# Query tiles inside the row norm, feed-forward tiles inside the output stage, and an earlier store of the last keys

## The reference

```
xn   = rmsnorm(x, norm1_w)
proj = xn @ w_in                  # q, k, v, forget logits, z, xBC, dt, two gates
q, k = headwise rmsnorm(q), headwise rmsnorm(k)      # 16 heads of 64
...                               # attention, state-space scan, branches -> merged
x = x + merged @ w_out
h = rmsnorm(x, norm2_w)
x = x + square(relu(h @ w_up)) @ w_down              # 1024 -> 4096 -> 1024
```

## Time and profile before

| what | value |
|---|---|
| median of 3 runs | 2817.95 us (2816.93 to 2821.05) |
| profiled execution | 2824.97 us |
| span of the profiled execution | 2823.2 us |
| mean granted clock of TensorE | 0.983 |
| PE busy in the span | 96% |
| DVE, ACT, POOL busy | 56%, 36%, 7% |

### The profile page before, as it was taken

The page is one execution under the profiler, slowest core; times in us unless marked ns, Lnnn a source line. Parts: engine busy times, 40 slices in busy tenths (PEclk is TensorE's granted clock), DMA queues, the critical chain, the costliest instruction groups (busy, mean ns, idle before and its releaser), DMA issues. The chain is left out here.

```text
span 2823.2 us, 47425 instructions
## 1 busy us (share of the span) xinstructions
PE 2715.8 (96%) x18594; PEld 2642.7 (94%) x18594; DVE 1581.2 (56%) x2975; ACT 1007.4 (36%) x2302; POOL 204.8 (7%) x299
## 2 busy tenths in 40 slices
PE   6999989999999999989999989999989999999999
PEld 5999979999999999979999989999989999999999
DVE  5444537657556567558998846454463444434434
ACT  4334336556565666543343422112221111111110
POOL 0000000000000000005555500000000000000000
PEclk8999999999999999999999999999989999999999
DMA  4441444243343343328888854333121111111112
GB/s 155 133 135 54 133 138 135 66 129 106 93 126 97 99 129 102 95 80 196 212 199 211 204 159 130 129 113 132 68 85 45 46 45 46 45 53 53 46 57 97
DMA packets 326606, 308.72 MB, mean 109 GB/s; under 512 B 66480, under 2 KB 283056, under 8 KB 326256
## 3 DMA queue, kind: packets, MB, share of 16 engines
q1 hardware_dynamic: 326384, 305.69, 36.9%
HBM read 218.32 MB, written 87.28 MB: 108 GB/s over the span
## 5 line engine op out<-in xcount | busy, mean ns | idle before, releaser
L411 PE MATMUL banks<-w_hi,xn_hi 128*128 128x256 f32 x1440 | 408.0, 287 | 5.0 <-DVEq L368 5.0
L411 PE MATMUL banks<-w_lo,xn_hi 128*128 128x256 f32 x1440 | 402.9, 284 | 0.0
L414 PE MATMUL banks<-xn_hi,w_hi 128*128 128x352 f32 x1152 | 380.2, 330 | 15.6 <-DVEq L368 8.3
L414 PE MATMUL banks<-xn_hi,w_lo 128*128 128x352 f32 x1152 | 379.6, 329 | 0.0
L414 PE MATMUL banks<-xn_lo,w_hi 128*128 128x352 f32 x1152 | 379.1, 329 | 0.0
L411 PE MATMUL banks<-w_hi,xn_lo 128*128 128x256 f32 x1280 | 364.0, 284 | 0.0
L411 PEld LDWEIGHTS banks<-w_hi,xn_hi 128*128 128x128 f32 x1440 | 274.5, 191 | 6.5 <-DVEq L368 5.1
L411 PEld LDWEIGHTS banks<-w_lo,xn_hi 128*128 128x128 f32 x1440 | 274.5, 191 | 0.1
L1862 PE MATMUL banks<-h_hi,w_hi 128*128 128x352 f32 x768 | 248.7, 324 | 2.3 <-DVEq L1783 2.3
L1862 PE MATMUL banks<-mlp_uhi,w_hi 128*128 128x352 f32 x768 | 248.5, 324 | 0.0
L1862 PE MATMUL banks<-h_hi,w_lo 128*128 128x352 f32 x768 | 248.4, 323 | 0.0
(11 more groups left out here) (282 smaller groups left out, 5906.7 us busy)
## 6 DMA issues: line engine op xcount, KB each, us to landing
w_raw<-in_w_in SPq DMA_DIRECT2D x44, 1024.0 KB, 5.6
scratch_xbc<-att_co SPq DMA_DIRECT2D x32, 512.0 KB, 2.7
ssd_ab<-scratch_acum SPq DMA_DIRECT2D x64, 256.0 KB, 5.8
br_g<-scratch_gates SPq DMA_DIRECT2D x72, 176.0 KB, 3.9
scratch_gates<-hand_tanh SPq DMA_DIRECT2D x48, 176.0 KB, 5.2
att_k<-scratch_k_hi SPq DMA_DIRECT2D x64, 128.0 KB
scratch_z<-att_z_stage SPq DMA_DIRECT2D x64, 128.0 KB, 2.0
ssd_xbc<-scratch_xbc SPq DMA_DIRECT2D x64, 128.0 KB, 3.3
```

The source lines that it names most:

```text
L411: ins = self.nc.tensor.matmul(self.bank(n, P, PW), x[:, k, t * P:(t + 1) * P], w[:, k, :], start=first, stop=end)
L414: ins = self.nc.tensor.matmul(self.bank(n, P, TT), w[:, k, m * P:(m + 1) * P], x[:, k, r * TT:(r + 1) * TT], start=first, stop=end)
```

## The change

In `norm_split` the q panel is loaded in quarters ahead of row tiles 2 to 8, ACT's table for the root is loaded by a first small instruction, and the order of ACT and DVE becomes root, scale, high and low one tile behind each other. PE multiplies each row tile of q (eight tiles, three times eight matmuls each) in the same stage, right after the turn of the next row tile. The eight products stay in banks 0 to 3, two to a bank; the turns use banks 4 to 7. The cached key rows and the k panel are loaded in this stage as well, and the k panel is split there.

`project_qkv` then begins with slot 8. Its slots 8 to 11 each empty two early tiles in front of the slot's own; the cached keys are turned in these slots; the norm of the first q panel follows three slots later than it would, and the groups of the first q and k panels two slots later. The v panel is loaded at once. Eight memsets move from DVE to POOL. The last k panel of a round is stored three slots behind its end.

In `out_norm`, slots 36 to 38 and the end take four tiles of the first up panel, in front of the last three turns and behind the last. The second up panel is loaded by slot 32, and the accumulator is cleared by DVE at slot 12. `mlp` leaves out these four tiles, and its up tiles of even panels go by pairs: both halves of the panel for one third of the rows.

```diff
-def norm_split(core, tag, srcs, hi, lo, norm_w, following):
+def norm_split(core, tag, srcs, hi, lo, norm_w, panels, cache_k, cache_rows):
...
+            load(0)
             sp.dma_start(wb[:], norm_w.to_broadcast([P, D])).then_inc(w_loaded, 16)
...
+            load(1)
+            for c, q in enumerate(quarters):
+                sp.dma_start(raw[:, q, :], panels[0].rearrange("(k p) m -> p k m", p=P)[:, q, :]).then_inc(p_loaded[c], 16)
+            for t in range(2, NT + 1):
+                load(t)
+            sp.dma_start(cache_rows, cache_k.rearrange("(t p) n -> p t n", p=P)).then_inc(cache_loaded, 16)
+            sp.wait_ge(p_lo, 4)
+            sp.dma_start(raw, panels[1].rearrange("(k p) m -> p k m", p=P)).then_inc(second_loaded, 16)
+            sp.wait_ge(cache_loaded, 16)
...
+            root(0)
+            root(1)
+            high(0)
+            for c, q in enumerate(quarters):
+                act.wait_ge(p_loaded[c], 16)
+                nc.scalar.activation(whi[0][:, q, :], raw[:, q, :], ACT.Copy).then_inc(p_hi, 1)
+            high(1)
+            root(2)
+            for t in range(3, NT + 1):
+                root(t)
+                high(t - 1)
+                if t >= NT - 3:
+                    if t == NT - 3:
+                        act.wait_ge(second_loaded, 16)
+                    q = quarters[t - NT + 3]
+                    nc.scalar.activation(whi[1][:, q, :], raw[:, q, :], ACT.Copy).then_inc(p_hi, 1)
+            high(NT)
...
+            scale(0)
+            scale(1)
+            low(0)
+            for c in range(4):
+                split_lo(0, c)
+            low(1)
+            scale(2)
+            for t in range(3, NT + 1):
+                scale(t)
+                low(t - 1)
+                if t >= NT - 3:
+                    split_lo(1, t - NT + 3)
+            low(NT)
...
+            def tile(t):
+                pe.wait_ge(lo_made, 2 * (t + 1))
+                tokens = slice(t * P, (t + 1) * P)
+                for k in range(KB):
+                    if t == 0 and k % 2 == 0:
+                        pe.wait_ge(p_lo, k // 2 + 1)
+                    for c, (x, w) in enumerate(((hi, whi[0]), (hi, wlo[0]), (lo, whi[0]))):
+                        nc.tensor.matmul(early_bank(core, t, P), x[:, k, tokens], w[:, k, :], start=k + c == 0, stop=k == KB - 1 and c == 2)
+            turn(0)
+            turn(1)
+            tile(0)
+            tile(1)
+            turn(2)
+            for t in range(2, EARLY_Q):
+                turn(t + 1)
+                tile(t)
+EARLY_Q = 8
+def early_bank(core, t, rows):
+
+    return core.banks[0:rows, t // 2, t % 2 * PW:(t % 2 + 1) * PW]
...
+    def drained(self, i, n):
+
+        if not (self.early and i == 0 and n < self.early + self.early // 2):
+            return [n]
+        u = n - self.early
+        return [2 * u, 2 * u + 1, n] if u >= 0 else []
...
-        if i == 0 and n % 2 and 0 <= n < 2 * self.CACHED:
-            out.append((n // 2, None))
+        c = n - self.stream.early
+        if i == 0 and 0 <= c < self.CACHED:
+            out.append((c, None))
...
-                if k in self.ended(n - 4 - g * self.stride(k)):
+                late = 2 if i == 0 and k < 2 else 0
+                if k in self.ended(n - 4 - late - g * self.stride(k)):
...
+        if i == 0 and n == self.stream.early:
+            dve.wait_ge(self.w_loaded, 48)
+            v.tensor_scalar(self.w_q[:], self.w_q[:], HD ** -0.5, None, ALU.mult).then_inc(self.cleared, 1)
...
-        for k in self.ended(n - 9):
-            if k % 2:
+        for k in range(1, self.per, 2):
+            if k in self.ended(n - (3 if k == self.per - 1 else 9)):
                 self.wait_normed(sp, i, k)
...
+        def up_tile(pe, u):
+
+            m, r = up_tile_of(0, u)
+            if u == 0:
+                pe.wait_ge(stream.lo_made, 4 * (len(panels) + 1))
+            stream.wait_free(pe, 0, LAST + 5 + u)
+            if u % 2 == 0:
+                pe.wait_ge(t_lo, 6 * (r + 1))
+            passes = [(x, w, k) for k in range(KB) for x, w in ((hi, stream.whi[0]), (hi, stream.wlo[0]), (lo, stream.whi[0]))]
+            for c, (x, w, k) in enumerate(passes):
+                nc.tensor.matmul(core.banks[:, u, 0:TT], w[:, k, m * P:(m + 1) * P], x[:, k, r * TT:(r + 1) * TT],
+                                 start=c == 0, stop=c == len(passes) - 1)
...
+                if n == LAST + 5:
+                    core.hold(sp, stream.lo_made, 4 * (len(panels) + 1))
+                    sp.dma_start(stream.raw, second.rearrange("(k p) m -> p k m", p=P)).then_inc(second_loaded, 16)
                 stream.sp(sp, 0, n, True)
...
                 if n < stream.slots:
                     stream.pe(pe, 0, n)
+                else:
+                    up_tile(pe, n - stream.slots)
                 t = turn_at(n)
...
+            up_tile(pe, EARLY - 1)
...
+                if n == ST + 3:
+                    nc.vector.memset(merged[:], 0.0).then_inc(cleared, 1)
...
+EARLY = 4
+def up_tile_of(j, t):
+
+    return (t % 2, t // 2) if j == 0 else (t // 3, t % 3)
...
-            nc.vector.memset(acc[:], 0.0).then_inc(cleared, 1)
             dve.sem_inc(free, NB)
...
+                        if s == 0 and n < EARLY:
+                            continue
```

More of the change, by code:

```diff
@@ new lines, in _, with root @@
+            nc.scalar.activation(junk[:, 0:1], core.ident[:, 0:1], ACT.Sqrt).then_inc(warmed, 1)
+            act.wait_ge(warmed, 1)
+            def root(t):
+                n = rows_of(t)
+                act.wait_ge(loaded[t], 16)
+                if t:
+                    act.wait_ge(summed, t)
+                nc.scalar.activation(junk[0:n, :], rows[0:n, t, :], ACT.Square, accum_out=ss[0:n, t:t + 1]).then_inc(summed, 1)
+                act.wait_ge(mean_made, t + 1)
+                nc.scalar.activation(ss[0:n, t:t + 1], ss[0:n, t:t + 1], ACT.Sqrt).then_inc(rooted, 1)
@@ new lines, in high @@
+            def high(t):
+                for i, blocks, bank in half_tiles(t):
+                    act.wait_ge(turned, i + 1)
+                    nc.scalar.activation(hi[:, blocks, t * P:t * P + rows_of(t)], bank, ACT.Copy).then_inc(hi_made, 1)
+            root(0)
[4 more added lines that the diff above has]
+                nc.scalar.activation(whi[0][:, q, :], raw[:, q, :], ACT.Copy).then_inc(p_hi, 1)
@@ L209, in _, with scale @@
             nc.vector.memset(hi[:, :, T + TS:TW].bitcast(F32), 0.0).then_inc(padded, 1)
-            def mean(t):
+            def scale(t):
                 n = rows_of(t)
@@ L312, in wait_free @@
     def wait_free(self, eng, i, n):
-        eng.wait_ge(self.free, len(self.banks) + i * self.slots + n + 1)
+        eng.wait_ge(self.free, len(self.banks) + i * self.slots + self.position(i, n) + 1)
     def epilogues(self):
@@ L373, in sp @@
         j, t = self.tiles[n]
-        if t == 4:
+        if t == 4 and not self.split_early(i, j + 1):
             self.load(sp, i, j + 2, last)
@@ L382, in act @@
             ep.act(act, i, n)
-        if t < 4:
+        if t < 4 and not self.split_early(i, j + 1):
             self.split_hi(act, i, j + 1, t)
@@ L402, in pe_part @@
                 pe.wait_ge(self.lo_made, 4 * (i * len(self.panels) + j + 1))
-            pe.wait_ge(self.free, i * self.slots + n + 1)
+            if not (self.early and i == 0 and n < self.early + len(self.banks)):
+                pe.wait_ge(self.free, len(self.banks) + i * self.slots + self.position(i, n - len(self.banks)) + 1)
         wh, wl = self.whi[j % 2], self.wlo[j % 2]
@@ L441, in act @@
                 act.wait_ge(self.stored, 48 * (i * self.per + k + 1))
+                if i + k == 0:
+                    act.wait_ge(self.norm.turned, self.norm.CACHED)
             s.wait_full(act, i, n)
@@ L486, in ended, with complete, tiles, order @@
         return [k for k, t in self.stream.mine(self, n) if t == NT]
+    def complete(self, i, n):
+        late = self.stream.early // 2 - 1 if i == 0 else 0
+        return [k for k in range(self.per) if k in self.ended(n - late * (k == 0))]
+    def tiles(self, i, n):
+        return [(m, k, t) for m in self.stream.drained(i, n) for k, t in self.stream.mine(self, m)]
+    def order(self, i):
+        return [(k, t) for n in range(self.stream.slots) for m, k, t in self.tiles(i, n)]
+    def before(self, i, k, t):
+        return i * self.per * (NT + 1) + self.order(i).index((k, t))
+    def whole(self, i, k):
+        return max(self.before(i, k, t) for t in range(NT + 1)) + 1
     def groups(self, i, n):
         out = []
-        if i == 0 and n % 2 and 0 <= n < 2 * self.CACHED:
-            out.append((n // 2, None))
+        c = n - self.stream.early
+        if i == 0 and 0 <= c < self.CACHED:
+            out.append((c, None))
         for g in range(self.GROUPS):
             for k in range(self.per):
-                if k in self.ended(n - 4 - g * self.stride(k)):
+                late = 2 if i == 0 and k < 2 else 0
```

(16 more changed lines are left out.)

194 lines of the change are left out of this document (93 added, 101 removed).

## The result

The median of four runs is 2798.77 us (2796.02 to 2800.31) against 2819.5 for the kernel before on the same chip (2816.93 to 2825.09): ratio 0.9923, 95% interval [0.9905, 0.994]. That is 20.7 us faster. The prediction was 2786 with a range up to 2797, so the direction was right and the gain was two thirds of the one forecast. From the 2817.95 that the forecast started at, the range's edge is a gain of 21.0, so the range was missed narrowly, but the sum of 31.85 by a third. The profiled execution took 2798.97, 26.0 less than the profiled execution before.

A forecast was written before the change was run, and what follows sets the result against it. PE, busy 96% of the span, was taken as the bound, so time could come only from its waits or lower clock. Gains of 16.0 + 2.9 + 12.95 = 31.85 us off 2817.95 gave 2786, range 2779 to 2797.

The forecast's parts named there:

- The k store: End of the projections: storing the last k panel earlier gains 2.9 us, bounds 0 and 5.6, at cost nothing.
- its own two terms, 1.8 and 1.2: Before attention: 1.8 us from fewer store issues ahead, 1.2 from the small store landing in 2.3 instead of 3.5.
- The sum: Whole kernel: 16.0 + 2.9 + 12.95 = 31.85 us gained, from 2817.95 to 2786.1.
- Row norm and slots 8 to 14: Row norm and early projections: eight early q tiles let slot 14 end at 72.4 instead of 88.46, 16.0 us gained.
- Rival 1: Slots 8 to 14: emptying three tiles per slot is slower, 1.6 us a round; 2791.4 us in all. Chance 0.14.
- The clock at the first tiles: Row norm: PE's clock rises at 19.5 us, with transposes from 13.5 on; tile 0 ends at 20.4.
- Rival 2: Row norm: clock rises only 5.8 us after the first real matmul tile; all 0.9 later, 2787 us. Chance 0.10.
- The output stage: Output stage's end into feed-forward: four early up tiles between the last turns keep PE dense, 12.95 us gained.
- rival 4: Output stage: turns wait behind early up tiles, the norm's last rows come late; 2796 us. Chance 0.06.
- rival 5: Feed-forward: new up-tile order makes PE wait over 4 us in each of eight slices; at 5, 2826 us. Chance 0.03.
- Rival 3: End of the projections: other transfers set the block's end, so the store's move gives nothing; 2789 us. Chance 0.07.

The follow-up runs named there:

- experiment 3: The kernel before with only the last k store moved to three slots behind, in both rounds: 2825.91 us, ratio 1.0014.
- experiment 4: The changed kernel again, unedited, as yardstick for other runs on the same chip: 2800.12 us, ratio 0.9918 to the kernel before.
- experiment 1: The changed kernel with round 0's last k store put back to nine slots behind: 2792.83 us, ratio 0.9893 to the kernel before.
- experiment 6: The changed kernel with output stage, feed-forward and k stores as before, leaving the row norm with early q tiles: 2808.02 us, ratio 0.9948.
- experiment 5: The kernel before with only the output stage's and feed-forward's part of the change: 2810.97 us, ratio 0.9957.
- experiment 7: The changed kernel with the accumulator's memset put back at the feed-forward's start: 2803.92 us, ratio 0.9934 to the kernel before.
- experiment 9: The changed kernel with round 0's load of the next weight panel three slots later: 2794.46 us, ratio 0.9894 to the kernel before.
- experiment 8: The changed kernel with round 0's full last k store issued by ScalarE on its own queue, four slots behind: 2796.56 us, ratio 0.9905.
- experiment 2: The changed kernel with round 0's early last k store cut to one row tile, 128 KB instead of 1 MB: 2794.73 us, ratio 0.9899.
- experiment 10: A second run of the changed kernel with round 0's last k store nine slots behind: 2790.42 us, ratio 0.9886.

## Why the prediction was wrong

**The k store** is the step that failed: "ACT wants its buffer back two groups on, 3 us later, and PE has three banks in hand: cost nothing." It was worked out from the last round, while the edit acts in both. In round 0 the moved megabyte meets the next weight panel's; at the 303 to 348 GB/s of that stretch 1 MB takes 3.0 to 3.5 us, the groups' stores land that much later, and the two buffers do not cover it. PE's three banks did not help either: what it waits for is the bank of the turns (DVE's subtraction, L685), and as its order is written out it stands before the turn until 186.65 and starts the next tile at 187.06 without a wait. The neighbours of the moved store should have been counted in each round. The forecast for the last round held: 3.0 us less waiting before attention in experiment 3 and 3.7 in the changed kernel, against 2.9 (its own two terms, 1.8 and 1.2, make 3.0). Round 0 costs 5.1 us in the trace of experiment 3 (matched operations go from 0.5 to 5.6 behind), 5.4 in the changed kernel's, 6.0 between experiments 4 and 1, and 7 by the ratios of these two. The term of +2.9 became -4 us (experiment 3: -1.4 to -6.5).

**The sum.** The three parts measured alone multiply to 0.9957 x 0.9948 x 1.0014 = 0.9919, which is the changed kernel's 0.9918; as far as intervals of some 4 us to either side can tell, they do not act on one another. In microseconds 12.1 + 14.7 - 4.0 = 22.8, where the forecast had 31.85. Of the 9 missing, 7 are the store's, 1.3 the row norm's and 0.9 the output stage's; the last two lie within what the intervals leave open. That the gain between the two profiled executions is 26.0 is partly chance: the one before, 2824.97, lies 5.5 above the median of 2819.5, and the last section shows 1.5 us of it.

**Row norm and slots 8 to 14.** 16.0 forecast, 15.7 to 16.9 between the traces at 92 us, 14.7 by experiment 6. The steps held: PE sets the pace from the third row tile, the block's change took 1.02 and not 1.6, and the waits fall at two cached groups and the first q group. Rival 1 (slower emptying) did not come.

**The clock at the first tiles.** Rival 2 put the rise at 21.2. In the nine traces it lies between 16.6 and 19.5, 1.2 to 4.1 us after the first real matmul, with two turns ahead of that; the forecast's 19.5 is the latest of them, and what places one execution in that stretch no run shows. The rule of the Trainium skill that stands there (TensorE: Matmul & The Clock Gate, Part 4: PE-mode transpose) would have had the turns do nothing for it; the traces differ from its 21.2 by 1.7 to 4.6 us.

**The output stage.** 12.95 forecast, 12.2 in the trace, 12.1 by experiment 5. Turns 6 and 7 did not delay the norm's rows (rival 4), the order of up tiles cost nothing in eight slices (rival 5), and the memset lay under other work, as experiment 7 shows from the other side: without that cover it costs 6.6, where the forecast said up to 7.1.

**Rival 3**, that the store's move gives nothing, was the nearest, for a reason that it did not name: in its own stretch the move gives 3, and loses more in a stretch that the prediction did not look at.

**What stays open.** At the output stage's start the first weight panel lands at slightly different times from one execution to the next: PE waits between 1.37 and 3.10 us there over the traces, in kernels with and without the output stage's part, and behind it the clock sometimes falls. The changed kernel's profiled execution lost 2.3 us there against before, and experiment 4's, the same kernel, lost 1.9 less than that. What sets the landing was not tried. Open too is what experiment 9 leaves: whether the small stores would pass the panel on another queue.

## What to carry to other kernels

An edit to a loop body acts in every round: cost a moved transfer in each round beside what that round loads and stores then, not only in the round for whose sake it is moved. A transfer that nobody waits for still costs when it delays small stores whose buffers are wanted soon; add up the bytes issued ahead of them and divide by the rate that the windows show. In experiment 8 a queue of its own for the large store gave back 0.9 of 6.0 us. Where the last round alone gains, do it in the last round alone: that version took 2790 to 2793 us, where the change as given took 2799 to 2800.

## What the runs showed of the hardware

The same pause brings the clock down in one execution and not in another. In the last round of the projections PE waits 1.68 or 1.69 us for the same subtraction in all twelve traces. First the kernel before, PE's timeline and windows, then the changed kernel:

```profile
282.29 0.28 PE L644 MATMUL banks<-ident,qkv_norm_stage 32*128 32x32 f32 x2 [1.69 <-DVE qkv_turned_lo L572]
...
284.00:286.00 2.00, 2.00 (x11) 2.00 (x11) 0.93 (x3) 1.01 (x2) 0.00 (x0) 0.50 0.99 347
286.00:288.00 2.00, 2.00 (x18) 2.00 (x18) 1.97 (x2) 0.39 (x1) 0.00 (x0) 0.96 0.38 78
```

```profile
271.04 0.28 PE L758 MATMUL banks<-ident,qkv_norm_stage 32*128 32x32 f32 x2 [1.69 <-DVE qkv_turned_lo L685]
...
272.00:274.00 2.00, 2.00 (x20) 2.00 (x19) 0.18 (x2) 1.71 (x4) 0.00 (x0) 1.00 0.98 354
274.00:276.00 2.00, 2.00 (x19) 2.00 (x18) 1.97 (x4) 0.38 (x1) 0.00 (x0) 1.00 0.45 136
```

The kernel before falls to 1.2 GHz and loses 1.5 us, in which the distance of matched operations goes from 11.3 to 12.7; the changed kernel stays at 2.4. The clock falls there in five of the twelve traces (before, experiments 2, 8, 9 and 10). At the output stage's start PE paused 3.10 us in experiment 7 and the clock stayed, 1.89 in experiment 2 and it fell. So a short wait has two prices, and 1.5 us between two single traces can be this alone.

In the changed kernel's row norm the clock column of the windows stands at 1.00 from 14 to 17 us, where PE's matmuls take 0.41 us as at 1.2 GHz: so early in the run the clock is read from the durations. The trace's own records of the clock begin at 17.1 us, and at 19.9 in the kernel before.
